# Two stacked float32r products for the scores, and inverse sums applied after the value product, in a two-layer hybrid encoder step

## The chip, the cores and the metric

One core of a Trainium2 chip runs the whole step. The metric is the device time of one execution in microseconds (us). The kernel before was run three times; the times given are the median and the extremes. The names used here: TensorE (PE) multiplies matrices, VectorE (DVE), ScalarE (ACT) and GpSimd (POOL) work on vectors, SyncE (SP) only issues transfers.

## The reference, cut to what matters

A two-layer encoder takes 1024 prompt frames and 8 streams of 16 frames. Each layer projects the normalised input into the operands of three groups of heads, attends, projects back and runs an MLP:

```
z = rmsnorm(x) @ W_in
A  "fox": 4 heads x 64, causal:      softmax(q k^T/8 + cum_q - cum_k) v      (forgetting attention)
B  "mla": 8 heads, q and k from latents, 64 + 32 rotary: softmax(q k^T / sqrt(96) + chunk mask) v
C  "swa": 4 q heads / 2 kv heads x 64, window of 3 chunks of 64, bias, a sink per head:
   softmax([q k^T/8 + bias, sink]) v
x = x + concat(A, B, C) @ W_out;   x = x + relu(rmsnorm(x) @ W_up)^2 @ W_down
```

Keys and values of the new frames are outputs too.

## The kernel before, in words

The frames are 9 tiles of 128 rows: 8 of the prompt and one with the 8 x 16 stream frames. Large products are made of three float32r (f32r) products, high x high, high x low and low x high: ScalarE rounds an operand to its high part, another engine subtracts to get the low part.

**Input projection.** The columns of W_in come in four slabs (512, 260, 416 and 512 wide), each in four weight pieces. Slab 0 holds fox queries and keys, slab 1 fox values and the forget gate, slab 2 the latents, slab 3 swa. Piece 4s+j of slab s is loaded by SP, rounded by ScalarE (in_hi, L1186) and its low part is made by VectorE (L1638) or GpSimd. ScalarE takes each product out of PSUM (evac_z); for slabs 0 and 3 into a staging tile, from which it issues the store of the keys (L1239) and which TensorE transposes a tile later (L2098, stg_bits). VectorE copies the transposed tile (stg_copy, L1649 to L1655) into qkTf or qkTs, [128, 4 or 3 planes, 1152 frames], where two heads share the 128 partitions of a plane. stg_copy runs inside VectorE's loop over tiles for slab 0, before the latents for six tiles of slab 3, and within the loop that normalises the latents (L1704, L1706) for the last three, at t = 2, 5 and 8.

**Latent stage.** After that loop VectorE copies the transposed latents (latT, L1716), ScalarE the rotary key (kTm, L1301), and TensorE sums the forget gates (L2188). SP meanwhile loads tables and masks and stores the new values, latents and gates, all from one queue, in written order.

**Prompt attention.** A hand-written list of 91 units per layer; a unit is some heads of one kind for one query tile (73 of them), or half of the tile's MLA query projection. Every engine walks the same list in steps. In step i TensorE transposes the probabilities of unit i-3 (LAG_T), multiplies the scores of unit i, and multiplies the values of unit i-4 (LAG). Transposed probabilities go in chunks of up to four 128 x 128 blocks through PSUM banks 4 and 5; VectorE copies even chunks (L1736), ScalarE odd ones (L1312), into ptb. In step i VectorE first copies its chunks, then normalises unit i-2 (LAG_N), and then takes the maxima of unit i. Normalising is one reciprocal of the row sums and, for each head, a multiply of its probabilities (L1748), and norm_ok releases the transposes. ScalarE takes the exponentials with row sums (sm_done) and copies the finished values out of PSUM (L1357) into omixT.

**Scores (L2237).** Queries and keys are plain f32. For fox and swa, whose planes hold two heads, GpSimd copies the queries of a tile into zero-padded planes (qzf, qzs; L1022, L1027), so that one product over 128 partitions sees one head alone. They are double buffered by tile.

## Time and profile before

| | us |
|---|---|
| three runs, median (extremes) | 2810.1 (2809.98 to 2814.61) |
| the profiled execution | 2807.96 |
| its span, first to last instruction | 2806.0 |
| TensorE busy in it | 2695.5 (96%) |
| mean granted TensorE clock | 0.989 |

The profile is of one execution. Busy time is per engine; an engine's idle time is put down to what released it. Only the idle time of an engine that everything waits for costs time. Matmuls are pipelined and their ends are modelled, so the start of one to the start of the next says more than a duration.

### The profile page before, as it was taken

How to read it: one execution, taken by the hardware profiler on the slowest of the kernel's cores; microseconds unless marked ns; L12 is line 12 of the kernel's file. 1: busy time of each engine (PE TensorE's matmuls, PEld its weight loads, DVE VectorE, ACT ScalarE, POOL GpSimd, SP SyncE). 2: the span in 40 equal slices, each digit the busy share in tenths (PEclk: the TensorE clock that was granted, in tenths of full speed). 3: DMA queues.
4: the chain of work that ended last, by engine and by line, in shares of the span. 5: the costliest groups of instructions: out<-in, count | busy, mean ns of one | idle time of the engine just before them, and what ended most of it. 6: DMA issues, size and time to landing. Idle time of an engine off the chain costs nothing.

```text
span 2806.0 us, 39617 instructions
## 1 busy us (share of the span) xinstructions
PE 2695.5 (96%) x14966; PEld 2177.9 (78%) x14966; DVE 1698.6 (61%) x2196; ACT 1054.8 (38%) x1969; POOL 1050.4 (37%) x594
## 2 busy tenths in 40 slices
PE   8999999899999999999999999998999999999997
PEld 6986666787888887888879756667878888878886
DVE  4026777635564558778740377775355564688777
ACT  4225544423323332333332255554243233333333
POOL 1112000114545457767511210001146444667766
PEclk9999999999999999999999999999999999999999
DMA  4212001432333446444132200013413433654441
GB/s 145 63 29 61 25 18 44 137 135 98 124 139 126 150 173 251 142 138 134 61 115 64 66 24 17 17 50 131 163 70 139 157 118 140 238 195 143 143 142 75
DMA packets 164722, 308.75 MB, mean 110 GB/s; under 512 B 24720, under 2 KB 90416, under 8 KB 164592
## 3 DMA queue, kind: packets, MB, share of 16 engines
q1 hardware_dynamic: 161280, 303.59, 31.4%
q10 hardware_dynamic: 3312, 3.41, 0.4%
q8 instruction: 84, 1.38, 0.2%
q14 instruction: 46, 0.38, 0.0%
HBM read 207.40 MB, written 97.72 MB: 109 GB/s over the span
## 4 chain that ended last, share of the span: by engine, by line
PE 86%; DVE 8%; ACT 2%; issue 2%; POOL 1%; DMA 1%; SPq 0%; DVEq 0%; ACTq 0%; POOLq 0%
PE ps L2583 8%; PE ps L2587 8%; PE ps L2585 8%; PE ps L2493 7%; PE ps L2494 7%; PE ps L2495 7%; PE ps L2237 6%; PE ps L2104 6%; PE ps L2106 6%; PE ps L2105 6%; PE ps L2098 5%; PE ps L2310 3%; PE ps L2370 2%; PE ps L2204 1%; PE ps L2438 1%
## 5 line engine op out<-in xcount | busy, mean ns | idle before, releaser
L2583 PE MATMUL ps<-wq_hi,sa_hi 128*128 128x512 f32 x896 | 349.0, 390 | 5.3 <-DVE x L2034 5.3
L2587 PE MATMUL ps<-wq_hi,sa_lo 128*128 128x512 f32 x896 | 348.6, 389 | 0.0
L2585 PE MATMUL ps<-wq_lo,sa_hi 128*128 128x512 f32 x896 | 348.6, 389 | 0.0
L2034 DVE TENSOR_TENSOR x<-ps,x 128x1024 f32<-128x1024 f32 x224 | 266.7, 1215 | 119.5 <-PE ps L2587 115.4
L1082 POOL TENSOR_TENSOR wq_lo<-wsum,wq_hi 128x1024 fp32r<-128x1024 f32 x64 | 157.5, 2462 | 289.7 <-ACT wq_hi L1454 289.7
L1972 DVE TENSOR_TENSOR sa_lo<-ra,sa_hi 128x1024 fp32r<-128x1024 f32 x112 | 253.3, 2263 | 19.8 <-ACT sa_hi L1474 19.7
L2104 PE MATMUL ps<-w_hi,hT_hi 128*128 128x512 f32 (+2 forms) x672 | 248.1, 369 | 0.3 <-DVE hT_lo L1643 0.3
L2106 PE MATMUL ps<-w_hi,hT_lo 128*128 128x512 f32 (+2 forms) x672 | 246.1, 366 | 0.0
L2105 PE MATMUL ps<-w_lo,hT_hi 128*128 128x512 f32 (+2 forms) x672 | 245.1, 365 | 0.0
L1964 DVE TENSOR_TENSOR cq<-ps,cq 128x1024 f32<-128x1024 f32 x48 | 58.6, 1221 | 285.4 <-ACT cq L1515 243.2
L2493 PE MATMUL ps<-hT_hi,wq_hi 128*128 128x512 f32 x512 | 203.2, 397 | 7.6 <-DVE hT_lo L1928 7.6
L1088 POOL TENSOR_TENSOR wq_lo<-rq,wq_hi 128x1024 fp32r<-128x1024 f32 x64 | 170.3, 2673 | 107.5 <-ACT wq_hi L1465 107.5
L2495 PE MATMUL ps<-hT_hi,wq_lo 128*128 128x512 f32 x512 | 201.5, 393 | 0.0
L2494 PE MATMUL ps<-hT_lo,wq_hi 128*128 128x512 f32 x512 | 201.3, 393 | 0.0
L2583 PEld LDWEIGHTS ps<-wq_hi,sa_hi 128*128 128x128 f32 x896 | 168.2, 188 | 41.6 <-issue 7.1
L994 POOL TENSOR_TENSOR w_lo<-w_raw,w_hi 128x1024 fp32r<-128x1024 f32 (+2 forms) x32 | 71.0, 2222 | 335.4 <-ACT w_hi L1186 335.4
L2587 PEld LDWEIGHTS ps<-wq_hi,sa_lo 128*128 128x128 f32 x896 | 168.2, 188 | 35.3
L2585 PEld LDWEIGHTS ps<-wq_lo,sa_hi 128*128 128x128 f32 x896 | 168.2, 188 | 34.7
L1082 POOL TENSOR_TENSOR wq_lo<-rq,wq_hi 128x1024 fp32r<-128x1024 f32 x64 | 170.6, 2676 | 57.7 <-ACT wq_hi L1454 57.2
L1088 POOL TENSOR_TENSOR wq_lo<-bsum,wq_hi 128x1024 fp32r<-128x1024 f32 x64 | 157.3, 2469 | 88.4 <-ACT wq_hi L1465 88.4
L1515 ACT COPY cq<-ps 128x512 f32<-128x512 f32 x128 | 73.4, 588 | 277.7 <-PE ps L2495 161.3
L2493 PE MATMUL ps<-T_hi,wq_hi 128*128 128x512 f32 x384 | 150.3, 391 | 1.5 <-POOL wq_lo L1082 1.4
(323 smaller groups left out, 6188.1 us busy)
## 6 DMA issues: line engine op xcount, KB each, us to landing
ra<-hidden_scratch SPq DMA_DIRECT2D x112, 512.0 KB, 3.3
hidden_scratch<-cq SPq DMA_DIRECT2D x94, 512.0 KB, 2.7
rq<-in_w_up_dram SPq DMA_DIRECT2D x64, 512.0 KB, 3.9
rq<-in_w_down_dram SPq DMA_DIRECT2D x64, 512.0 KB, 4.3
residual_scratch<-x SPq DMA_DIRECT2D x27, 512.0 KB, 3.1
x<-residual_scratch SPq DMA_DIRECT2D x27, 512.0 KB, 7.3
x<-in_x_prompt_dram SPq DMA_DIRECT2D x16, 512.0 KB, 6.9
w_raw<-in_w_in_dram SPq DMA_DIRECT2D x16, 512.0 KB, 4.2
```

Source lines behind the costliest of these rows:

```text
L1082: nc.gpsimd.tensor_tensor(wq_lo[o % 4][:], up_source(o)[:], wq_hi[o % 4][:], ALU.subtract).then_inc(up_lo.sem, 1)
L1088: nc.gpsimd.tensor_tensor(wq_lo[k][:], down_b_source(o)[:], wq_hi[k][:], ALU.subtract).then_inc(b_lo.sem, 1)
L2034: nc.vector.tensor_tensor(part, bank(b0 + 2 * pair, 2).rearrange("p (t n) -> p t n", t=2), part, ALU.add).then_inc(dn_ev.sem, 1)
L2104: pe.matmul(out, ah, bh, start=(k == 0), stop=False)
L2105: pe.matmul(out, ah, bl, start=False, stop=False)
L2106: last = pe.matmul(out, al, bh, start=False, stop=(k == n - 1))
L2493: pe.matmul(out, wh[:, cols], h[:, k, :], start=new and k == 0, stop=False, skip_group_check=True)
L2494: pe.matmul(out, wh[:, cols], lo_h[:, k, :], start=False, stop=False, skip_group_check=True)
L2495: last = pe.matmul(out, wl[:, cols], h[:, k, :], start=False, stop=k == 3, skip_group_check=True)
L2583: pe.matmul(out, ah[:, k, :], bh[:, k * 512:(k + 1) * 512], start=new and k == 0, stop=False, skip_group_check=True)
L2585: pe.matmul(out, ah[:, k, :], bl[:, k * 512:(k + 1) * 512], start=False, stop=False, skip_group_check=True)
L2587: last = pe.matmul(out, al[:, k, :], bh[:, k * 512:(k + 1) * 512], start=False, stop=final and k == 1, skip_group_check=True)
```

## The change

1. **Scores.** For fox and swa one f32 product becomes two f32r products. VectorE's stg_copy makes a high part (rounded to f32r) and a low part (a subtraction) for tiles 0 to 7. A new tensor keysF (keysS) holds for every key head the high part in partitions 0 to 63 and the low part in 64 to 127; queriesF (queriesS) holds the query's high part twice (j = 0) and its low part twice (j = 1). So (q_hi, q_hi) against (k_hi, k_lo), plus (q_lo, q_lo) against the same, is the whole product. The parts get into place by transfers that ScalarE issues in store_split: per tile two stores of queries to scratch in DRAM and four moves of keys within SBUF. SP loads the stacked queries back, tile by tile. The tile of the streams is copied plainly into newF and newS, after all stores of its kind have landed. The padding by GpSimd goes.
2. **Softmax.** L1748 goes. VectorE makes the reciprocal only; GpSimd spreads it over 64 columns per head (ginv); TensorE transposes it with the unit's probabilities as extra "inverse" blocks; VectorE multiplies the value product by the transposed inverse into omixT, in place of ScalarE's L1357. Of a unit with more than two chunks the first two are transposed ahead of the next scores, the others behind.
3. MLA units have at most four heads (tile 0 had one of eight), and the final norm uses signals that exist.

The core of the diff:

```diff
 def tile_units(kind, t):
-    n = min(HEADS[kind], 1024 // head_stride(kind, t))
+    n = min(HEADS[kind], 4, 1024 // head_stride(kind, t))
...
+def inverse_blocks(u):
+    _, _, h0, heads = UNITS[u]
+    return heads // 2 if heads > 1 else h0 % 2
...
     blocks = [(g, b) for g in range(UNITS[u][3]) for b in key_blocks(u)]
+    blocks += [("inverse", k) for k in range(inverse_blocks(u))]
...
# SP
+                for i in range(2):
+                    sp.wait_ge(split_out[i].sem, split_out[i].at(l, 2 * SPLIT_TILES))
+                load_queries("fox", 0)
                 sp.wait_ge(kpe_ev.sem, kpe_ev.at(l, NPT))
                 load(kTm[64:96, 1:MLA_H, :], kTm[64:96, 0:1, :].broadcast_to([ROPE, MLA_H - 1, NPT * P]), kpe_all)
+                sp.wait_ge(lat_ev.sem, lat_ev.at(l, NT))
+                sp.wait_ge(prep_out.sem, prep_out.at(l, 16 * 10))
+                load_queries("swa", 0)
                 for t in range(NPT - 1):
+                    for kind in ("fox", "swa"):
+                        sp.wait_ge(sc_mm.sem, sc_mm.at(l, scores_behind(kind, t)))
+                        load_queries(kind, t + 1)
                     sp.wait_ge(o_ev.sem, o_ev.at(l, TILE_END[t]))
...
# POOL
+                for u, n in ATTN.items():
...
+                    pool.wait_ge(inv_ok.sem, inv_ok.at(l, n + 1))
...
+                    nc.gpsimd.tensor_copy(ginv[:, m % 4, g0:g0 + heads, :],
+                                          rinv[:, n % 4, 0:heads].unsqueeze(2).broadcast_to([P, heads, HD])
+                                          ).then_inc(spread_ok.sem, 1)
...
# ACT
+                def store_split(kind, t):
+                    m = t if kind == "fox" else NT + t
+                    act.wait_ge(stg_ev.sem, stg_ev.at(l, m + 1))
...
+                    done = split_out[t % 2]
+                    for j in range(2):
+                        part = (split_hi, split_lo)[j][kind][t % 2]
+                        act.dma_start(query_d[kind][t, :, j, :], part[:, 0:2, :]...).then_inc(done.sem, 16)
+                        for r in range(2):
+                            rows, half = slice(64 * r, 64 * r + 64), slice(64 * j, 64 * j + 64)
+                            if kind == "fox":
+                                act.dma_start(keysF[half, r:FOX_H:2, toks[t]], part[rows, 2:4, :].bitcast(F32)).then_inc(done.sem, 16)
+                            else:
+                                act.dma_start(keysS[half, r, toks[t]], part[rows, 2, :].bitcast(F32)).then_inc(done.sem, 16)
...
                     if t >= 1:
                         evac_z(t - 1)
+                    if t >= 4:
+                        store_split("fox", t - 4)
...
                 for s in range(1, 4):
...
+                    if s == 1:
+                        store_split("fox", 5)
                     in_hi(4 * s + 2)
+                    if s == 1:
+                        store_split("fox", 6)
                     in_hi(4 * s + 3)
+                    if s == 1:
+                        store_split("fox", 7)
...
                         evac_z(s * NT + t)
+                        if s == 3 and t >= 3:
+                            store_split("swa", t - 3)
...
+                store_split("swa", 6)
+                store_split("swa", 7)
                 for t in range(NT):
                     act.wait_ge(lat_ev.sem, lat_ev.at(l, t + 1))
...
# DVE
                 def stg_copy(m):
...
+                    if t == NPT:
+                        for i in range(2):
+                            dve.wait_ge(split_out[i].sem, split_out[i].at(l, SPLIT_TILES * (1 if m < NT else 2)))
+                        nc.vector.tensor_copy(new[:], src[:, 0:planes, :]).then_inc(stg_ev.sem, 1)
+                        return
+                    if t >= 2:
+                        dve.wait_ge(split_out[t % 2].sem, split_out[t % 2].at(l, splits_stored(kind, t - 2)))
+                    chain.link(nc.vector.tensor_copy(high, src[:, 0:planes, :]))
+                    nc.vector.tensor_tensor(low, src[:, 0:planes, :], high, ALU.subtract).then_inc(stg_ev.sem, 1)
...
-                        if t == NT + 1:
+                        if t == NT:
                             lo(6, 0, 2 * SLABS_IN[1][1])
                             lo(7, 1, 2 * SLABS_IN[1][1])
...
-                        chain.link(nc.vector.reciprocal(inv, sums))
-                        for g in range(heads):
-                            probs = pbuf[n % 4][:, g * w:(g + 1) * w]
-                            last = nc.vector.tensor_scalar(probs, probs, inv[:, g:g + 1], None, ALU.mult)
-                        last.then_inc(norm_ok.sem, 1)
+                        nc.vector.reciprocal(inv, sums).then_inc(inv_ok.sem, 1)
...
+                    if i >= LAG and group_ending(i - LAG) is not None:
...
+                        dve.wait_ge(pv_mm.sem, pv_mm.at(l, n + 1))
+                        nc.vector.tensor_tensor(omixT[t % 2][:, c0:c0 + pairs, :].rearrange("p k n -> p (k n)"),
+                                                bank(6 + n % 2)[:, 0:pairs * P],
+                                                ptb[ch % NPTB][:, i0:i0 + pairs * P],
+                                                ALU.mult).then_inc(o_ev.sem, 1)
...
# PE
+                            qs, keys = [queriesF[:, h % 2, j, h // 2, :].bitcast(F32R) for j in range(2)], keysF[:, h, :].bitcast(F32R)
...
-                            last = pe.matmul(out[:, c0:c1], q, keys[:, k0 + c0:k0 + c1], start=True, stop=not masked)
+                            for j, q in enumerate(qs):
+                                last = pe.matmul(out[:, c0:c1], q, keys[:, k0 + c0:k0 + c1], start=(j == 0),
+                                                 stop=(j == len(qs) - 1 and not masked))
...
-                    pe.wait_ge(norm_ok.sem, norm_ok.at(l, n + 1))
+                    pe.wait_ge(sm_done.sem, sm_done.at(l, u + 1))
...
+                            if g == "inverse":
+                                if b == 0:
+                                    pe.wait_ge(spread_ok.sem, spread_ok.at(l, n + 1))
+                                src = ginv_b[:, GROUP_OF[u] % 4, 2 * b:2 * b + 2, :].rearrange("p h d -> p (h d)")
...
-                        probs_transposes(i - LAG_T)
+                        probs_transposes(i - LAG_T, slice(0, 2))
                     if 3 <= i < len(UNITS):
                         scores(i)
+                    if transposing and len(chunks_of(i - LAG_T)) > 2:
+                        probs_transposes(i - LAG_T, slice(2, None))
```

## Rows read from the trace of the kernel before

**Rows 1.** The page's first lines: span, busy time and share of each engine.

```profile
span 2806.0 us, 39617 instructions
PE 2695.5 (96%) x14966; PEld 2177.9 (78%) x14966; DVE 1698.6 (61%) x2196; ACT 1054.8 (38%) x1969; POOL 1050.4 (37%) x594
```

**Rows 2.** Busy time by stretches: us, five engines with counts, TensorE clock, DMA share, GB/s.

```profile
200.00:220.00 20.00, 15.02 (x112) 14.40 (x110) 15.19 (x25) 3.03 (x12) 10.06 (x13) 0.83 0.69 180
220.00:518.00 298.00, 279.70 (x2091) 186.49 (x2092) 214.26 (x529) 155.91 (x422) 14.73 (x37) 0.99 0.12 35
1610.00:1908.00 298.00, 279.85 (x2097) 186.79 (x2096) 214.20 (x530) 155.91 (x422) 14.23 (x35) 0.99 0.12 35
```

**Rows 3.** Groups of TensorE instructions, 220 to 518 us: busy, mean ns | idle before.

```profile
L2098 PE MATMUL ps<-identR,pbuf_bits 128*128 128x128 f32 x492 | 60.0, 262 | 13.7 <-DVE pbuf L1748 11.3 <-ACT ptb L1312 2.1
```

**Rows 4.** The same view for VectorE and ScalarE, 220 to 518 us.

```profile
L1748 DVE TENSOR_SCALAR pbuf<-pbuf,rinv 128x256 f32<-128x256 f32 (+7 forms) x128 | 56.2, 476 | 2.6
L1748 DVE TENSOR_SCALAR pbuf<-pbuf,rinv 128x128 f32<-128x128 f32 x16 | 3.7, 298 | 0.1
L1736 DVE COPY ptb<-ps 128x512 f32<-128x512 f32 x72 | 49.4, 686 | 20.0 <-PE ps L2098 19.9
L1357 ACT COPY omixT<-ps 128x128 f32<-128x128 f32 (+2 forms) x49 | 14.1, 287 | 5.6 <-PE ps L2310 5.6
```

**Rows 5.** Timeline of TensorE: start, duration, line, tiles, shape, count.

```profile
234.31 7.13 PE L2254 MATMUL ps<-wukv,latT 128*128 128x512 f32 x16
260.93 0.88 PE L2098 MATMUL ps<-identR,pbuf_bits 128*128 128x128 f32 x8
261.64 3.69 PE L2237 MATMUL ps<-kTm,qTm 104*128 104x256 f32 x16
...
1452.05 0.46 PE L2104 MATMUL ps<-w_hi,hT_hi 128*128 128x512 f32 x1
1457.61 0.46 PE L2098 MATMUL ps<-identR,stg_bits 128*128 128x128 f32 x4
```

**Rows 6.** ScalarE's transfers of staged keys: ns min/median/max, first and last start, landing.

```profile
L1239 ACTq DMA_DIRECT2D out_dram<-stg x22: 338/338/411, 29.9 to 1591.3; - x22
...
DMA to landing us min/median/max: 1.5/1.7/8.7
```

**Rows 7.** Timeline of layer 1 where slab 1 starts, all engines.

```profile
1471.26 1.15 ACT L1186 CAST w_hi<-w_raw 128x520 fp32r<-128x520 f32 x2 [0.47 <-ACT stg L1223]
1471.99 1.44 DVE L1638 TENSOR_TENSOR w_lo<-w_raw,w_hi 128x520 fp32r<-128x520 f32 x2 [0.79 <-ACT w_hi L1186]
1472.74 0.39 PE L2133 MATMUL ps<-w_hi,hT_hi 128*128 128x260 f32 x1 [0.77 <-DVE w_lo L1638]
```

**Rows 8.** Timeline of layer 0's latent stage, all engines.

```profile
201.85 0.34 ACTq L1239 DMA_DIRECT2D out_dram<-stg  x1
201.90 8.08 SPq L661 DMA_DIRECT2D qTm<-const_mask_mla_q_dram  x2
206.45 0.54 DVE L1655 COPY qkTs<-ps 128x384 f32<-128x384 f32 x1
206.91 0.54 DVE L1716 COPY latT<-ps 128x384 f32<-128x384 f32 x1
207.89 0.70 PE L2098 MATMUL ps<-identR,zc_bits 128*128 128x128 f32 x4 [3.03 <-ACT kTm L1301]
225.56 0.49 PE L2237 MATMUL ps<-qkTf,qzf 128*128 128x128 f32 x2
```

**Rows 9.** Duration (ns min/median/max) of lines near to the added operations.

```profile
L1653 DVE COPY qkTf<-ps x18: 691/692/694, 36.0 to 1474.8; 128x512 f32<-128x512 f32 x18
L1027 POOL COPY qzf<-qkTf x32: 391/401/493, 219.8 to 1766.5; 64x256 f32<-64x256 f32 x32
```

**Rows 10.** DMA issues: transfer, queue, count, KB each, median us to landing.

```profile
out_dram<-stg ACTq DMA_DIRECT2D x4, 64.0 KB, 4.8
```

More of the change, by code:

```diff
@@ L476, in hybrid_step @@
         max_done = signal("max_done", NATTN)
-        qz_ok = signal("padded_queries_copied", 2 * NPT)
+        split_out = [signal(f"split_stored{i}", 2 * SPLIT_TILES) for i in range(2)]
+        queries_in = {kind: signal(f"queries_in_{kind}", 32 * NPT) for kind in ("fox", "swa")}
         has_waited = signal("dve_has_waited", 0)
@@ L1016, in _ @@
                                             ALU.mult).then_inc(lb_ok.sem, 1)
-                def pad_zeros(bufs, other):
-                    for buf in bufs:
-                        for r in range(2):
-                            nc.gpsimd.memset(buf[64 * r:64 * r + 64, other(1 - r), :], 0.0)
-                def pad_queries(dst, src, planes, t):
-                    for r in range(2):
-                        rows = slice(64 * r, 64 * r + 64)
-                        last = nc.gpsimd.tensor_copy(dst[t % 2][rows, planes(r), :], src[rows, 0:2, toks[t]])
-                    last.then_inc(qz_ok.sem, 1)
@@ L1348, in _ @@
                                        ).then_inc(wk_ev.sem, 1)
-                    if i >= LAG and group_ending(i - LAG) is not None:
-                        n = group_ending(i - LAG)
-                        kind, t, h0, _ = UNITS[GROUPS[n][0]]
-                        pairs = sum(UNITS[u][3] for u in GROUPS[n]) // 2
-                        act.wait_ge(pv_mm.sem, pv_mm.at(l, n + 1))
-                        if t >= 2 and n == TILE_END[t - 1]:
-                            act.wait_ge(mix_out[t % 2].sem, mix_out[t % 2].at(l, 16 * (t // 2)))
-                        c0 = {"fox": 0, "mla": 2, "swa": 6}[kind] + h0 // 2
-                        nc.scalar.copy(omixT[t % 2][:, c0:c0 + pairs, :].rearrange("p k n -> p (k n)"),
-                                       bank(6 + n % 2)[:, 0:pairs * P]).then_inc(o_ev.sem, 1)
                 def mix_high(t):
@@ L1789, in attention_step @@
                                                             ALU.subtract).then_inc(max_done.sem, 1)
+                    if i >= LAG and group_ending(i - LAG) is not None:
+                        n = group_ending(i - LAG)
+                        kind, t, h0, _ = UNITS[GROUPS[n][0]]
+                        pairs = sum(UNITS[u][3] for u in GROUPS[n]) // 2
+                        ch, i0 = inverse_place(i - LAG)
+                        if ch % 2:
+                            dve.wait_ge(pt_act.sem, pt_act.at(l, ch // 2 + 1))
+                        if t >= 2 and n == TILE_END[t - 1]:
+                            dve.wait_ge(mix_out[t % 2].sem, mix_out[t % 2].at(l, 16 * (t // 2)))
+                        c0 = {"fox": 0, "mla": 2, "swa": 6}[kind] + h0 // 2
+                        dve.wait_ge(pv_mm.sem, pv_mm.at(l, n + 1))
[3 more added lines that the diff above has]
+                                                ALU.mult).then_inc(o_ev.sem, 1)
                 for n in range(0, 24, 2):
@@ L2387, in stream_scores @@
                                     else:
-                                        last = add(S[rows, 256:384], q, qkTf[:, 2 + c, new], stop=(c == 1))
+                                        last = add(S[rows, 256:384], q, newF[:, 2 + c, :], stop=(c == 1))
                     elif kind == "swa":
@@ L2396, in stream_scores @@
                                 else:
-                                    last = add(S[rows, 128:256], q, qkTs[:, 2, new], stop=True)
+                                    last = add(S[rows, 128:256], q, newS[:, 2, :], stop=True)
                     else:
```

144 lines of the change are left out of this document (81 added, 63 removed).

## The prediction

> **What bounds the kernel now.** I began with the page's busy shares: TensorE is busy 2695.5 of 2806.0 us, 96%, and no other engine passes 61% [rows 1]. So an edit counts by what it does to TensorE's instructions and to the 110 us in which it stands still. The busy time by stretches of layer 0 says where that is [rows 2]: the latent stage (200 to 220) leaves 5.0 of 20 us idle at a granted clock of 0.83 (a mean; 1 is the upper level, 2.4 GHz), and the prompt attention (220 to 518) leaves 18.3 of 298 us. Layer 1's attention repeats this with 18.2, so I work out one layer and double it.
>
> Inside the attention the groups of TensorE instructions name the loss [rows 3]: 13.7 us stand before the transposes of the probabilities, and VectorE's normalising line L1748 released 11.3 of them. VectorE has 128 of those instructions, 56.2 us, beside its 49.4 us of copies [rows 4].
>
> **Part 1, the inverse sums.** VectorE loses the 56.2 us of L1748, ScalarE the 14.1 us of L1357 [rows 4]. Neither bounds the stretch, so this is worth only the wait it removes. The transposes now wait for the exponentials (sm_done), not the scaling: I take the whole 13.7 us as gone; 18.3, all idle time, is the upper end. What comes in:
> - TensorE transposes 64 "inverse" blocks. Eight transposes start 0.71 us ahead of what follows [rows 5], so one is 0.09 us: +5.8 us.
> - 26 more chunk copies (170 for 144), alternating between VectorE and ScalarE, at most 0.69 each, and 50 multiplies of values by inverses on VectorE. A small L1748 is 0.30 us, a 512-wide VectorE tensor operation that reads PSUM 0.69 [rows 4, 9]: 15 to 35 us. VectorE falls from 214 to some 182 to 202 of 298 us, so it still doesn't bound.
> - GpSimd's 74 spreads, 0.40 us each by its nearest row [rows 9], are hidden: it is busy 14.7 of 298 us. In its queue only the table fills after the last tile stand behind a waiting spread.
> - VectorE's wait for the values product ends its step; behind it stands the next step's chunk copy, for which transposes wait. Cover is the product itself, which TensorE runs last in that step. I cost this at nothing and keep half of the 13.7 us as the lower end (second rival).
>
> **Part 2, the score products.** 160 f32 products per layer become 320 f32r ones. Sixteen f32 products of 512 columns take 7.13 us, less 0.17 of modelled tail: 435 ns each. Twenty-four f32r products start 5.56 us before what follows them: 232 ns [rows 5]. A pair costs 464, 29 ns more: +4.6 us. MLA's f32 products stay. So part 1 and these pairs give 13.7 - 5.8 - 4.6 = 3.3 us of gain (ends: 6.9 - 10.4 = -3.5, and 18.3 - 10.4 = +7.9).
>
> Here a rule says otherwise. The Trainium skill, page "FP8 and Floating Point Precision", section "TensorE Precision Notes", gives true FP32 four passes through the array; by it two one-pass products would halve the time of one. The rows' ratio of the two is 1.9, so I price by the rows; the halving stands below as a rival.
>
> **Part 3, making the split.** Per tile VectorE's copy becomes a copy and a subtraction, 0.69 each [rows 9], and ScalarE issues six transfers. One issue takes 0.338 us, the landing typically 1.7 us from the issue [rows 6]: six hold ScalarE for 2.03 us. 96 go out per layer. In three places something waits.
> - A, start of slab 1. Now ScalarE rounds both weight pieces at 1471.26, VectorE subtracts at 1471.99, and TensorE has already stood still 0.77 us at 1472.74 [rows 7]. Six issues now stand before the first rounding and six before the second. VectorE's second subtraction ends 2 x 2.03 us later, about 0.2 hides in the present gap: +3.9 us. Nothing covers this; TensorE's order has no other work here.
> - B, end of slab 3. VectorE's normalising loop contains the last three staging copies. Now the last one runs at 206.45, the first latT copy at 206.91, and TensorE resumes at 207.89, behind ScalarE's kTm copy, after 3.03 us [rows 8]. In the changed kernel the copy of tile 7 waits for the stores of tile 5, issued after ScalarE's transfer at 201.85, so from 202.2 to 204.25. SP's mask loads issue from 201.90 to 210.0 [rows 8]; the longest landing of the staged keys' stores, 8.7 us, is of one issued here [rows 6]. I take the landing as 210; then 1.2 us for the pair of tile 7 (0.54 each, and their hand-over), 2.03 us for its own six transfers, an ordinary 1.7 us landing: the last staging copy, which waits for every store, starts at 215.0 in place of 206.45: +8.5 us. With ordinary landings throughout it is 204.25 + 1.4 + 1.2 + 2.05 + 1.7 = 210.6: +4.2. If tile 7's stores land beside SP's 1 MB store in 4.8 us, the median of the four 64 KB ones [rows 10], it is +11.6.
> - C, slab 0. The copy of tile t waits for the stores of tile t-2. The step is 6.5 us; an ordinary landing leaves it just in time: +0.4 (0 to 5, if four steps stall 1.2 us each).
>
> By the Trainium skill, page "DMA: Bandwidth & Descriptors", section "Issuing engines are not separate DMA queues", all issuers' transfers interleave on the same 16 engines and the sequencer's time is usually small beside the transfer. Then A would be near 0 and B 4.2, the sum 8.2 us smaller per layer. The rows speak against it for 64 KB pieces: 2.03 us of issue against 1.4 us from the issue's end to the landing.
>
> **What costs nothing.** The first fox queries are loaded from SP's queue behind the logf stores and are wanted at 225.56 [rows 8], both moved by B alike. SP's two waits for the splits stand in front of the kTm broadcast, wanted only by the MLA units. Later query loads wait for the scores of the tile before, with the other heads' units for cover, and hold back only the mix stores. MLA tile 0 as two units of four moves no work. The final norm's signals are only renamed.
>
> **Sum per layer:** A 3.9 + B 8.5 + C 0.4 - 3.3 = +9.5 us, +19.0 for two. The profiled run took 2807.96 us (span 2806.0, 1.96 outside) and lies 2.1 under the median of 2810.1. So 2827.0 against the profiled run, 2829 against the median: 0.7% slower.
>
> **Rivals.**
> - Faster: the transposes' wait is worth more than its idle time. Their 492 records add up to 60.0 us [rows 3], against 44.3 at 0.09 us each; the 15.7 us between may be waiting inside modelled ends. If half of it is, part 1 and 2 gain 18.3 + 7.9 - 10.4 = 15.8 per layer and the sum is 12.8 - 15.8 = -3.0: 2804, or 2796 with B at 4.2. It decides from 15.6 us of gain. Against it: modelled ends of pipelined instructions overlap anyhow. Chance 0.11.
> - Slower still: the wait for the inverse spread and VectorE's wait for the values take half of the old wait's place. 12.8 + 3.5 = 16.3 per layer: 2843. For it: VectorE already waits 19.9 us for transposes before its chunk copies [rows 4], so the two take turns. Chance 0.13.
> - No measurable difference: ordinary landings (B 4.2) and all idle time gone (7.9): +0.6 per layer, 2811. Chance 0.16.
> - The score products do halve. 52,224 columns (counted from the list of units) at 435/512 ns are 44.4 us per layer; a saving of 22.2 in place of a cost of 4.6 gives -17.3: 2775. Chance 0.02, as an f32r product would have to fall from 232 to 109 ns. This is what the first page's rule would give.
>
> **How the numbers follow.** The forecast, A and B as worked out, has the remaining 0.58: 2829. A measurement of this kernel can tell about 0.2%, 5.6 us, from no change: faster is 0.11 + 0.02 = 0.13, same 0.16, slower 0.58 + 0.13 = 0.71. The range runs from 2804 (the faster rival's nearer end) to 2848: 2843, and 2.4 us more per layer of the 3.1 by which B can exceed 8.5. Left out are 0.02 below, half of the first rival and some 0.1 above. Slower cases alone: 2816 to 2848.
>
> **What would show it.** Right: ScalarE's rounding at slab 1 some 2 and 4 us later with TensorE idle behind VectorE's subtraction; the first latT copy 4 to 12 us later behind a staging copy that waits for a transfer; f32r score pairs at 464 ns; idle time before the transposes well under 13.7 us. Wrong: slab 1 without a gap, latT copies within 2 us of now, or a new releaser (GpSimd's spread, VectorE's multiply) with more than 7 us before transposes or values.

## The result, and the profile after

The changed kernel takes 2858.9 us (median of four runs, 2858.0 to 2861.8) against 2812.4 us for the kernel before in the same comparison (2810.0 to 2815.3): a ratio of 1.0167, interval 1.0149 to 1.0184. It is slower, as forecast, but by 46.6 us where 19 were forecast, and outside the range. The profiled execution took 2861.83 us, span 2860.0, mean granted clock 0.974 (before: 2807.96, 2806.0, 0.989). The page's first lines, after, against [rows 1]:

```profile
span 2860.0 us, 40455 instructions
PE 2700.9 (94%) x15094; PEld 2208.9 (77%) x15094; DVE 1628.1 (57%) x2102; ACT 1056.7 (37%) x1897; POOL 1057.7 (37%) x662
```

TensorE's busy time rose by 5.4 us only, the span by 54.0. So by the page almost all of the loss is idle time. That sum hides two opposite changes, and a table by stage shows them. I built it from both timelines, taking as bounds the starts of TensorE's instructions that both kernels have (first product of a slab, first product of the streams' tile in slab 3, first product with wuq, the transposes of wukv at the attention's end, the first product of the mix), in us, layer 0 / layer 1. The last column is the part of the difference that is idle time of TensorE:

| stage | before | after | difference | of it idle |
|---|---|---|---|---|
| slab 0 | 63.4 / 60.7 | 70.0 / 67.1 | +6.6 / +6.4 | +4.4 / +3.9 |
| slab 1 | 27.2 / 27.2 | 36.8 / 36.8 | +9.6 / +9.6 | +6.0 / +6.3 |
| slabs 2 and 3 | 87.3 / 87.3 | 87.3 / 87.3 | 0 | 0 |
| latent stage | 24.6 / 24.5 | 38.8 / 40.0 | +14.2 / +15.5 | +13.7 / +13.8 |
| prompt attention | 289.4 / 289.3 | 277.5 / 275.2 | -11.9 / -14.1 | +0.3 / +1.1 |
| streams' attention | 71.0 / 71.0 | 80.7 / 79.3 | +9.7 / +8.3 | -1.0 / -0.9 |
| the rest | 824.6 / 836.5 | 825.0 / 835.4 | +0.4 / -1.1 | +0.1 / 0 |

With the 0.7 us ahead of layer 0's first product the layers add up to +29.3 and +24.7, the span's difference. Four stages lose, the attention gains. In the attention TensorE works some 12 to 15 us less, in slabs 0 and 1 and the streams' stage some 15 to 17 us more; the page's total shows neither.

**Slab 1 (A).** The timeline of layer 1 after, ScalarE's queue and then TensorE, against [rows 7]; a "q" marks an issue of a transfer, the bracket is idle time and who ended it:

```profile
1506.87 0.45 ACTq L1279 DMA_DIRECT2D query_scratch_fox<-splitF_hi  x1
1507.35 1.26 ACTq L1284 DMA_DIRECT2D keysF<-splitF_hi  x2
1508.65 0.61 ACTq L1279 DMA_DIRECT2D query_scratch_fox<-splitF_lo  x1
1509.29 1.26 ACTq L1284 DMA_DIRECT2D keysF<-splitF_lo  x2
1510.64 0.62 ACT L1210 CAST w_hi<-w_raw 128x520 fp32r<-128x520 f32 x1 [4.19 <-issue]
...
1514.58 0.63 ACT L1210 CAST w_hi<-w_raw 128x520 fp32r<-128x520 f32 x1 [3.31 <-issue]
```

```profile
1512.13 0.58 PE L2197 MATMUL ps<-w_hi,hT_hi 128*128 128x260 f32 x1 [4.50 <-DVE w_lo L1682]
...
1516.06 0.59 PE L2197 MATMUL ps<-w_hi,hT_hi 128*128 128x260 f32 x1 [2.26 <-DVE w_lo L1682]
```

The mechanism is the one forecast: six issues before each rounding, VectorE's subtraction behind it, TensorE idle. The price is not. From 1506.87 to the rounding at 1510.64 the six take 3.77 us, 0.63 each, where I had 0.338. And idle time is not all: the windows of slab 1 in layer 1, before and after, show the granted clock at 0.86 in place of 1.00 and TensorE 3.3 us longer at the same products. From within the first of the two waits on it stood at 0.50 for 10.2 us, so of the 9.6 us lost 6.3 are idle time and 3.3 are clock.

```profile
1470.30:1497.50 27.20, 26.43 (x223) 26.21 (x223) 2.79 (x4) 6.72 (x21) 3.96 (x2) 1.00 0.23 68
```

```profile
1505.97:1542.78 36.81, 29.72 (x222) 29.00 (x222) 4.77 (x7) 6.72 (x21) 3.96 (x2) 0.86 0.34 94
```

**Slab 0 (C).** VectorE's split waits for the transfers of two tiles earlier. The transfers' own line says how often, and the timeline shows one of them:

```profile
L1284 ACTq DMA_DIRECT2D keysF<-splitF_hi x32: 603/623/1884, 50.3 to 1518.4; - x32
...
  DVE splitF_hi L1705: 52.0, 10
```

```profile
1490.03 0.69 DVE L1705 CAST splitF_hi<-ps 128x512 fp32r<-128x512 f32 x1 [5.59 <-DMA keysF<-splitF_lo]
```

The median issue is 623 ns; ten splits waited 5.2 us each on average. TensorE feels it as a wait for the low parts of the next tile's input: 4.3 us in three waits in layer 1 after, 0.3 us before.

**Latent stage (B).** The timeline of layer 0 after, VectorE, ScalarE, SP and TensorE, against [rows 8]:

```profile
218.78 8.15 SPq L691 DMA_DIRECT2D qTm<-const_mask_mla_q_dram  x2
228.18 0.56 DVE L1705 CAST splitS_hi<-ps 128x384 fp32r<-128x384 f32 x1 [6.62 <-DMA keysS<-splitS_lo]
229.72 2.80 ACTq L1286 DMA_DIRECT2D keysS<-splitS_hi  x2
232.56 1.35 ACTq L1279 DMA_DIRECT2D query_scratch_swa<-splitS_lo  x1
238.26 0.56 DVE L1700 COPY newS<-ps 128x384 f32<-128x384 f32 x1 [6.96 <-DMA keysS<-splitS_lo]
239.72 0.70 PE L2162 MATMUL ps<-identR,zc_bits 128*128 128x128 f32 x4 [13.55 <-ACT kTm L1355]
```

This is the forecast's chain: tile 7's split waits for tile 5's transfers until 228.18, its own six issues run from 229.36 to 235.21, the last copy starts at 238.26, and TensorE resumes after 13.55 us where it had 3.03. The six took 5.85 us, where I had 2.03. SP issues its masks from 218.78 on, in 8.15 us, and tile 5's last transfers, issued by 222.60, land 5.5 to 5.8 us after their issue; those of the tiles before mostly land 1.2 to 1.4 us after it.

**Attention.** Groups of TensorE's instructions in layer 0, after (251 to 530 us), against [rows 3], then the score groups of before (220 to 510 us):

```profile
L2162 PE MATMUL ps<-identR,pbuf_bits 128*128 128x128 f32 x492 | 60.3, 260 | 6.0 <-ACT ptb L1366 4.3 <-DVE ptb L1787 1.3
L2303 PE MATMUL ps<-keysF,queriesF 128*128 128x512 f32 (+3 forms) x96 | 23.7, 367 | 0.0
L2303 PE MATMUL ps<-keysS,queriesS 128*128 128x256 f32 (+1 forms) x64 | 9.4, 290 | 0.7 <-issue 0.7
L2162 PE MATMUL ps<-identR,ginv_bits 128*128 128x128 f32 x64 | 17.6, 312 | 4.4 <-issue 3.6 <-ACT pbuf L1387 0.6
L2383 PE MATMUL ps<-ptb,Vf 128*64 128x128 f32 x288 | 18.8, 277 | 2.3 <-ACT ptb L1366 2.1 <-issue 0.2
```

```profile
L2237 PE MATMUL ps<-qkTf,qzf 128*128 128x512 f32 (+3 forms) x96 | 37.2, 508 | 0.6 <-ACT pbuf L1333 0.6
L2237 PE MATMUL ps<-qkTs,qzs 128*128 128x256 f32 (+1 forms) x64 | 15.3, 382 | 0.7 <-issue 0.7
```

Read the counts first: 96 and 64 in both kernels, though the code now issues two products where it issued one. So **one f32 product is two records** in this profile. Before, 96 records were 48 fox products (four heads, and 12 pieces of at most 512 columns for each over the eight tiles); now they are 48 pairs. And the groups' busy time fell, from 37.2 to 23.7 and from 15.3 to 9.4 us. One head's 896 columns against one query tile show it, before and after:

```profile
417.31 1.74 PE L2237 MATMUL ps<-qkTf,qzf 128*128 128x512 f32 x4
418.88 0.22 PE L2239 MATMUL ps<-cmaskB,identB 128*128 128x128 bf16 x1
```

```profile
439.80 1.05 PE L2303 MATMUL ps<-keysF,queriesF 128*128 128x512 f32 x4
440.69 0.23 PE L2306 MATMUL ps<-cmaskB,identB 128*128 128x128 bf16 x1
```

From the start of the scores to the start of the mask it is 1.57 us as f32 (two pieces, four records) and 0.89 us as pairs (four products, four records).

**Streams' attention.** The forecast has no term for this stage. Busy time of it, before and after (us, five engines, clock, DMA share, GB/s):

```profile
509.36:580.35 70.99, 64.98 (x563) 56.06 (x562) 38.46 (x106) 29.44 (x75) 10.02 (x13) 1.00 0.31 106
```

```profile
528.55:609.24 80.69, 75.73 (x561) 64.89 (x562) 37.13 (x107) 29.03 (x74) 9.80 (x13) 0.85 0.28 93
```

The same instructions, 10.75 us more of them busy, at a clock of 0.85 in place of 1.00. Idle time hardly moved (6.0 to 5.0 us): this part of the loss is clock. It stands at 0.50 for 23.9 us of this stage, and before for none.

### The profile page after: what moved, and what is told of

Same layout as the page of the kernel before. It is cut to its first block, busy times and chain, and to the rows that moved or that the text cites. A ratio compares the mean times of both kernels' runs of the same rounds, so it can differ in the third digit from the quotient of the medians.

```text
span 2860.0 us, 40455 instructions
## 1 busy us (share of the span) xinstructions
PE 2700.9 (94%) x15094; PEld 2208.9 (77%) x15094; DVE 1628.1 (57%) x2102; ACT 1056.7 (37%) x1897; POOL 1057.7 (37%) x662
## 4 chain that ended last, share of the span: by engine, by line
PE 81%; issue 5%; DVE 5%; ACT 2%; ACTq 2%; DMA 2%; POOL 2%; SPq 0%; DVEq 0%; POOLq 0%
PE ps L2659 8%; PE ps L2663 8%; PE ps L2661 8%; PE ps L2569 7%; PE ps L2570 7%; PE ps L2571 7%; PE ps L2168 5%; PE ps L2170 5%; PE ps L2169 5%; PE ps L2162 5%; PE ps L2303 5%; PE ps L2383 4%; PE ps L2446 2%; PE ps L2268 1%; PE ps L2514 1%
## 5 line engine op out<-in xcount | busy, mean ns | idle before, releaser
L1073 POOL COPY ginv<-rinv 128x64 f32<-128x64 f32 (+2 forms) x148 | 41.2, 278 | 513.4 <-DVE rinv L1798 513.4
```

## The experiments

The kernel before was run again beside each set: 2813.1 us in the first, 2812.2 in the second, 2811.9 in the third. All times are medians unless said otherwise.

**First set: which part costs what.** *split_only*: the changed kernel with part 2 of the change taken back, that is normalising by VectorE as before, no inverse blocks, no spreads, ScalarE's copy into omixT; the limit of four heads for MLA and the new order of the transposes go back with it.

```diff
-                        nc.vector.reciprocal(inv, sums).then_inc(inv_ok.sem, 1)
+                        chain.link(nc.vector.reciprocal(inv, sums))
+                        for g in range(heads):
+                            probs = pbuf[n % 4][:, g * w:(g + 1) * w]
+                            last = nc.vector.tensor_scalar(probs, probs, inv[:, g:g + 1], None, ALU.mult)
+                        last.then_inc(norm_ok.sem, 1)
...
-                    pe.wait_ge(sm_done.sem, sm_done.at(l, u + 1))
+                    pe.wait_ge(norm_ok.sem, norm_ok.at(l, n + 1))
```

> The changed kernel with the inverse part undone: VectorE normalises the probabilities again (128 multiplies per layer), no inverse blocks, no spread, ScalarE copies the values out; the f32r pairs and everything that makes them stay. Theory (the pairs halve the score time, making the split is what costs): the input projection and the latent stage lose 31 us per layer as in the changed kernel, fox and swa scores gain some 20 us per layer, the wait for the normalising stays as before; the stream stage keeps its full clock. About 2812 + 2 x 11 = 2834 us. Rival (the inverse part made the gain in the attention, the pairs cost 4.6 us): about 2812 + 2 x 36 = 2884 us.

It took 2851.1 us, 1.0142 (1.0125 to 1.0159). Slabs 0 and 1 and the latent stage are as slow as in the changed kernel (67.8, 36.8, 39.2 us), the streams' stage is nearly as before (72.4, 72.6), and the attention is already 9.8 us faster than before (279.6, 279.5). The gain in the attention is mostly the pairs'. The total is 17 us above the 2834 expected, mainly because some 20 us per layer were expected there and 9.8 came: TensorE is busy 18.1 us less in it (254.9 for 273.0), but idle 8.2 us more (24.6 for 16.4).

*inverse_only*: the kernel before with the inverse part alone; plain f32 scores, padding by GpSimd between its spreads.

```diff
-                    pe.wait_ge(norm_ok.sem, norm_ok.at(l, n + 1))
+                    pe.wait_ge(sm_done.sem, sm_done.at(l, u + 1))
...
+                            if g == "inverse":
+                                if b == 0:
+                                    pe.wait_ge(spread_ok.sem, spread_ok.at(l, n + 1))
+                                src = ginv_b[:, GROUP_OF[u] % 4, 2 * b:2 * b + 2, :].rearrange("p h d -> p (h d)")
```

> The kernel before with the inverse part alone: zero-padded f32 queries by GpSimd as before, no split; sums inverted, spread by GpSimd, transposed with the probabilities, multiplied into the values by VectorE. Theory: 64 more transposes cost 5.8 us per layer and the idle time only moves from the normalising to the chunk copies and the inverse blocks, so the attention is 5 to 8 us longer per layer: 2822 to 2828 us, and 2841 to 2847 if the clock falls behind the attention here too. Rival (the removed wait pays): 13.7 - 5.8 = 8 us gained per layer, 2796 us.

It took 2823.8 us, 1.0036 (1.0016 to 1.0056). That is within the 2822 to 2828 expected, but by luck: the attention, which was to lose 5 to 8 us per layer, gained 0.5 in one and lost 1.5 in the other (288.9 and 290.8 us). The clock did fall behind it, for which 2841 to 2847 us was expected: the streams' stage takes 79.4 and 79.3 us. Groups of TensorE's instructions, 220 to 509 us:

```profile
L2134 PE MATMUL ps<-identR,pbuf_bits 128*128 128x128 f32 x492 | 60.0, 260 | 5.8 <-ACT ptb L1345 5.1 <-DVE ptb L1759 0.3
...
L2134 PE MATMUL ps<-identR,ginv_bits 128*128 128x128 f32 x64 | 16.7, 297 | 3.3 <-issue 2.5 <-ACT pbuf L1366 0.6
```

The idle time before the transposes falls from 13.7 to 5.8 us, but TensorE's whole idle time in the attention only from 16.4 to 13.5 us in layer 0 (288.9 less 275.4 busy) and from 16.3 to 12.4 in layer 1: the rest turns up before inverse blocks, values and MLA scores. TensorE's busy time rises by 2.4 and 5.4 us with 64 more transposes, so the two about cancel.

*sp_splits*: the changed kernel with the split's transfers issued from SP's queue, between its loads of weight pieces, and none from ScalarE's.

```diff
 # SP
-                for i in range(6, PC_IN):
+                for k in range(4):
+                    store_split("fox", k)
+                piece(6, in_piece(l, 1, 2))
+                store_split("fox", 4)
+                store_split("fox", 5)
+                piece(7, in_piece(l, 1, 3))
+                store_split("fox", 6)
...
+                for k in range(NPT):
+                    store_split("swa", k)
 # ACT
-                    if t >= 4:
-                        store_split("fox", t - 4)
...
```

> The changed kernel with the 96 transfers per layer issued from SP's queue, each tile's six as soon as VectorE has made its parts, none from ScalarE. Theory (ScalarE's issues and the stores that start late are the cost): slab 0 and the start of slab 1 return to the times of before, the latent stage to within 3 us, so 25 to 30 us are back per layer: 2800 to 2809 us. Rival (VectorE's second operation and the landings are the cost, whoever issues): more than 2840 us.

It took 2819.5 us, 1.0027 (1.0017 to 1.0037): some 39 of the 46.6 us are back with the queue, yet it is 10 us above the expected range. Slab 0 takes 63.4 and 61.1, slab 1 27.2, the latent stage 24.3 and 26.2 us, all within 2 us of before. The transfers and their bytes are the same, and so is the time of an issue: a median of 0.60 us on SP's queue as on ScalarE's. Two more things change with the queue, though. SP issues a tile's six as soon as its parts are made, and its masks go out behind the last of them, so that landings in the latent stage are back at 1.2 to 1.4 us from the issue's end. What each of the three is worth in slab 0 and in the latent stage this run doesn't separate. One new wait shows in TensorE's timeline of layer 0, the first scores waiting for the first queries from scratch, which SP loads behind its stores:

```profile
232.71 0.66 PE L2303 MATMUL ps<-keysF,queriesF 128*128 128x128 f32 x2 [7.03 <-DMA queriesF<-query_scratch_fox]
```

With it the attention takes 284.2 and 283.5 us, and the streams' stage is as slow as in the changed kernel (80.6, 77.2): that is what the expectation left out.

*warm*: the changed kernel with 12 more transposes, into a bank that is overwritten, where TensorE waits for ScalarE's wukT at the attention's end.

```diff
+                    for k in range(12):
+                        turned(bank(2, 2)[:, k % 8 * P:(k % 8 + 1) * P], wukv_b[:, k % 8].rearrange("p e d -> p (e d)"))
                     pe.wait_ge(wk_ev.sem, wk_ev.at(l, 1))
```

> The changed kernel with 12 more transposes of a resident tile, into a PSUM bank that is rewritten afterwards, where TensorE stands still 1.1 us for ScalarE's wukT copy at the end of the attention. Theory (the lower clock level at the start of the stream stage is set off by the idle time at the end of the attention): the granted clock stays at 1.00 behind it and the stream stage is 9 to 10 us shorter per layer: about 2840 us. Rival (the clock falls there whatever TensorE does in that gap, or falls later): 2857 to 2861 us, clock again near 0.85 in the stream stage.

It took 2849.6 us, 1.0133 (1.0116 to 1.015), against 1.0167; 2840 was expected. The profile is of the slowest of the four executions (2857.5), and in it the streams' stage takes 80.4 and 77.6 us, so it doesn't show where the other three gained. The first fall of the clock was gone, but it fell some us later, behind two short waits for ScalarE's kcT (0.72 and 0.79 us). One filled gap isn't the whole of it.

**Second set: what is queued behind VectorE's new wait, and the parts together.** *qlat_first*: the changed kernel, but in the attention's last step VectorE copies qpeS and the latent queries ahead of its wait for the last values product; the copies' later places go.

```diff
+                    if i == len(UNITS) + LAG - 1:
+                        nc.vector.tensor_copy(qpeS[0:ROPE].rearrange("p s h q -> p h s q"),
+                                              qTm[0][64:96].rearrange("p h (s q) -> p h s q", s=STREAMS)
+                                              ).then_inc(st_q.sem, 1)
+                        dve.wait_ge(ql_mm.sem, ql_mm.at(l, 1))
+                        nc.vector.tensor_copy(qlat[:].rearrange("p s h q -> p h s q"),
+                                              bank(2, 2).rearrange("p (h s q) -> p h s q", h=MLA_H, s=STREAMS)
+                                              ).then_inc(ql_ev.sem, 1)
                     if i >= LAG and group_ending(i - LAG) is not None:
```

> The changed kernel with one order on VectorE put back: in the last step of the attention it copies the stream queries (qpeS) and the latent queries (qlat) before it waits for the last values product, not behind it. Theory (TensorE stands still longer at the start of the stream stage because the latent queries stand behind VectorE's new wait, and that is where the clock is lost): one idle stretch of 0.6 to 0.8 us less per layer; if the clock then stays at its upper level the stream stage is 9 us shorter per layer, 2840 us; if the gap for wukT still sets it off, 2857 us. Rival (the order does not matter): 2857 to 2861 us and the clock again near 0.86 there.

It took 2849.9 us, 1.0132 (1.0114 to 1.015). That is halfway between the 2840 and the 2857 expected. The streams' stage falls to 75.1 and 77.7 us, its clock rises to 0.93 in layer 0. TensorE's wait of 0.66 us there, which the kernel before doesn't have, is gone, and so is the fall of the clock behind it; the fall behind the wait for wukT stays, and a short one comes later, from 553.4 on.

The next three take *sp_splits*' queue with one more step: SP waits for the splits and loads the first queries right behind the band, ahead of the stores of Vf and the rest. *sp_early_split* does that to *split_only*; *sp_early_qlat* to the changed kernel, with *qlat_first*'s edit; *sp_early_qlat_warm* adds *warm*'s.

```diff
 # SP, behind the load of the band
+                for i in range(2):
+                    sp.wait_ge(split_out[i].sem, split_out[i].at(l, 2 * SPLIT_TILES))
+                load_queries("fox", 0)
```

> The f32r pairs alone (VectorE normalises the probabilities as before, no inverse blocks), with the split's transfers issued by SP as soon as each tile is made, and the first fox queries loaded back before SP's stores of values, latents and gates. Theory (pairs halve the score products, ScalarE's issues were the cost, the inverse part only costs): projection and latent stage as before, attention 9.8 us shorter per layer as in the run with the pairs alone, stream stage within 2 us of before: 2812 - 16 to 20, 2792 to 2797 us. Rival (the split costs elsewhere too, for instance by VectorE's second operation): 2805 us or more.

> Both parts of the change, with SP issuing the split's transfers, the first fox queries loaded early, and VectorE's copies of the stream and latent queries put before its last values multiply. Theory: projection and latent stage as before, attention 12 us shorter per layer; stream stage 71 us if the clock holds (2786 us), 79 us if it does not (2802 us). Rival (the inverse part is worth keeping only if the attention is shorter than with the pairs alone): not below the run with the pairs alone.

> The same as the last with 12 more transposes in TensorE's gap before the latent queries. Theory (with both gaps closed the clock stays at its upper level): stream stage 71 us, about 2786 us, and below the run without the transposes if that one loses its clock. Rival (clock falls all the same): 2800 us or more.

They took 2796.1 us, 0.9944 (0.9927 to 0.9961); 2797.0 us, 0.9948 (0.9931 to 0.9964); and 2791.2 us, 0.9925 (0.9908 to 0.9941). All three beat both kernels; the last is the lowest of the study, though its interval overlaps the others'. The wait of 7.03 us is gone (latent stages 24.2 to 25.8 us). Where the first two differ is instructive: *sp_early_split* has 280.2 and 281.6 us in the attention and 72.6 and 70.8 in the streams' stage, *sp_early_qlat* 275.2 and 276.9, and 75.9 and 74.1. With VectorE's copies early, the inverse part earns about 5 us in the one stage and loses about 3 in the other; in the medians nothing of that is left (the second profile is of the fastest of its four executions, 2791.3). With *warm*'s transposes that stage is at 70.8 and 74.7. The page's head of the last kernel, and its streams' stage by windows in both layers:

```profile
span 2788.6 us, 40503 instructions
PE 2677.6 (96%) x15118; PEld 2189.9 (79%) x15118; DVE 1636.2 (59%) x2102; ACT 1056.1 (38%) x1897; POOL 1057.4 (38%) x662
```

```profile
498.43:569.27 70.84, 66.01 (x573) 57.08 (x574) 38.37 (x107) 28.96 (x74) 9.87 (x13) 1.00 0.32 106
1877.32:1951.98 74.66, 70.47 (x573) 60.79 (x574) 36.34 (x107) 28.87 (x74) 9.94 (x13) 0.93 0.30 101
```

**Third set: two questions left.** *late_stores*: the changed kernel with the three sets of issues at slab 1's start behind both roundings, still on ScalarE.

```diff
-                    if s == 1:
-                        store_split("fox", 5)
                     in_hi(4 * s + 2)
-                    if s == 1:
-                        store_split("fox", 6)
                     in_hi(4 * s + 3)
                     if s == 1:
-                        store_split("fox", 7)
+                        for t in range(5, NPT):
+                            store_split("fox", t)
```

> The changed kernel with one order on ScalarE altered: at the start of slab 1 it rounds both weight pieces first and issues the 18 transfers of fox tiles 5, 6 and 7 behind them. Theory (term A is ScalarE's issues ahead of the roundings): TensorE's wait for the weight pieces, 7.7 us, goes; the 18 issues, some 11.4 us, still keep ScalarE from taking slab 1's products out of PSUM, and two banks cover about 6 us of that: slab 1 takes 30 to 33 us in place of 36.8, 8 to 14 us less in all, 2845 to 2851 us. Rival (the slab is late because the landings are late): slab 1 stays at 36 to 37 us, 2857 to 2861 us.

It took 2863.8 us, 1.0174 (1.0151 to 1.0198), no better than the changed kernel, where 2845 to 2851 was expected; slab 1 takes 37.0 and 38.0 us. (The wait that was to go, 7.7 us in the expectation, is 6.8 in the rows of slab 1: 4.50 and 2.26.) TensorE in layer 1:

```profile
1507.22 0.39 PE L2194 MATMUL ps<-w_hi,hT_hi 128*128 128x260 f32 x1 [0.78 <-DVE w_lo L1679]
...
1520.38 0.59 PE L2165 MATMUL ps<-w_hi,hT_hi 128*128 128x260 f32 x1 [8.22 <-ACT ffz L1266]
```

The wait for the low parts is back to 0.78 us, as in [rows 7], and in its place TensorE waits 8.22 us until ScalarE, busy issuing, has taken the tile's products out of PSUM. So the outcome is about the rival's, but not for its reason, late landings: ScalarE was on the path of this stage at both places of the issues that were tried.

*one_product*: *sp_early_split* without the second product of each pair, so that the low parts of fox and swa queries are left out. This line is added for fox and for swa:

```diff
+                            qs = qs[:1]
```

> The pairs alone, issued by SP, as in the run with early queries, with the second product of each pair (the low parts of the queries) left out. Theory (a product of 512 f32r columns takes 232 ns, and 26,112 columns per layer are left out): fox and swa records halve, the score instructions of fox and swa take 11.8 us less per layer, and the attention is 5 to 12 us shorter than 281 us, as far as VectorE lets it: 2772 to 2786 us. Rival (a product costs what one record suggested, so that 52,224 columns are left out): 23 us less per layer in the score instructions.

One run: 2801.8 us, where 2772 to 2786 was expected. Groups of TensorE's instructions in the attention, *sp_early_split* and then this:

```profile
L2130 PE MATMUL ps<-identR,pbuf_bits 128*128 128x128 f32 x492 | 59.4, 261 | 19.4 <-DVE pbuf L1780 17.0 <-ACT ptb L1337 2.2
...
L2271 PE MATMUL ps<-keysF,queriesF 128*128 128x512 f32 x48 | 15.8, 429 | 0.0
```

```profile
L2130 PE MATMUL ps<-identR,pbuf_bits 128*128 128x128 f32 x492 | 60.8, 265 | 26.1 <-DVE pbuf L1780 23.7 <-ACT ptb L1337 2.2
L2273 PE MATMUL ps<-keysF,queriesF 128*128 128x512 f32 x24 | 10.2, 463 | 0.0
```

Half the products are half the records, 24 for 48: an f32r product is one record. The attention didn't get shorter, 280.4 and 280.5 us against 280.2 and 281.6. TensorE is busy 9.0 us less in layer 0 and idle 9.2 us more, most of it as a longer wait for VectorE's normalising, 17.0 to 23.7 us. With the pairs in, and without the inverse part, TensorE's work no longer sets the length of this stage. The streams' stage takes 75.6 us in both layers, 10.2 of them at a clock of 0.50, in an execution without the inverse part.

## Why the prediction was right in sign and wrong in size

Slower was right, and A, B and C are where it said. The forecast +9.5 us per layer stands against +29.3 in layer 0: A, B and C cost 17.6 more than forecast, the attention gave 8.6 more, and 9.7 came from a stage without a term. The sign is in part luck. Had only the pairs been priced right (20.7 saved, see part 2), the sum would have read 12.8 - 28.6 = -15.8 per layer, faster; two errors in opposite directions kept it right.

**The price of an issue (A, B and C), the step that failed first.** "One issue takes 0.338 us" came from [rows 6], where each issue stands by itself. Back to back they take 0.60 to 0.63 us in the median. It is not the kind of transfer: the same store of queries takes 0.44 us (fox) and 0.33 (swa) as the first of its six, 0.61 and 0.60 as the fourth. Single ones take longer, 1.3 to 1.5 us where SP issues at the same time in the latent stage, and up to 2.07 elsewhere. A measured 9.6 for 3.9, B 14.2 and 15.5 for 8.5, C about 6.5 for 0.4. B even passed its upper end of 11.6: in layer 0 its last staging copy came 6.4 us later than forecast, 3.8 by its own six issues (5.85 us for 2.03) and some 1.3 by each of the two landings. C passed its upper end of 5. The price of an issue is not all of A and C either. The sum had only idle time in it, but 3.3 to 3.6 us of A and 2.2 to 2.5 of C are TensorE working longer at the lower clock. *sp_splits* shows that issuing them on ScalarE is the cause of all three: the same transfers from SP's queue, at the same 0.60 us each, bring the three stages back. For A, where the order on ScalarE was tried as well, it is the time that ScalarE spends; for B and C that time, the late place in its order and B's meeting with SP's masks are not told apart.

The Trainium skill, page "DMA: Bandwidth & Descriptors", section "Issuing engines are not separate DMA queues", holds the sequencer's time for usually small beside the transfer. I weighed that rule and set it aside, and the runs go further against it: six issues took 3.77 us against 2.1 from a fox key's issue to its landing, and changing the queue was worth 39 us.

**Part 2, wrong in sign.** "Sixteen f32 products of 512 columns take 7.13 us ... 435 ns each": these were 16 records, and eight products of 870 ns. The same mistake made 160 products of 80, and the count of columns twice too large. A pair at 464 ns does not cost 29 more, it saves 406. By columns: 4 heads x 36 key blocks x 128 for fox and 4 x 15 x 128 for swa are 26,112, so 44.4 us become 23.7, 20.7 saved per layer against +4.6 forecast. The groups' busy time fell by 19.4 us (52.5 to 33.1), which agrees. So the rival to which I gave 0.02, that the score products halve, has the mechanism right; its argument against, that an f32r product would have to fall to 109 ns, rested on the same misreading. The Trainium skill, page "FP8 and Floating Point Precision", section "TensorE Precision Notes", gives true FP32 four passes through the array; the rows give 870 / 232 = 3.75 to 1, so the measurement comes near the page's four.

**Part 1, wrong in size.** I took the 13.7 us of idle time as gone. *inverse_only* shows that 3 to 4 us of TensorE's idle time go and the attention gains nothing. VectorE's normalising was one of several things that hold up the transposes; with it gone the chunk copies come last (5.4 of 5.8 us in the rows of *inverse_only*), and 3.3 us turn up before the inverse blocks, for most of which the rows name no releaser. The sign named beforehand, idle time before the transposes well under 13.7 us, came true without the gain that it stood for. On its own the part's net, +0.5 and -1.5 us, was near the lower end I kept (6.9 - 5.8 = 1.1). Only with the pairs in does it earn, about 2 to 5 us, since VectorE's normalising is then what is late.

**Why 20.7 us of cheaper scores gave 10.** *split_only* and *one_product* answer: a shorter product makes TensorE wait longer, mostly for VectorE. In *split_only* 18.1 us of work went and 8.2 us of idle time came; in *one_product* the next 9.0 us bought nothing. Pairs alone gave 9.8 us, and both parts 11.9 and 14.1. That is the sum "13.7 - 5.8 - 4.6 = 3.3" replaced: neither price was right, and the two gains don't add.

**The streams' stage, left out.** The sentence that failed is "VectorE's wait for the values product ends its step; behind it stands the next step's chunk copy ... I cost this at nothing". In the last step no chunk copy stands behind it but the copies of the streams' queries. Both layers lose, in *inverse_only* too (8.4 and 8.3 us), and hardly in *split_only* (1.4 and 1.6): it comes mostly with the inverse part. Not all of it does, as *one_product* loses 4.6 in each layer without that part. TensorE's timeline in layer 0 after, and the clock by windows around the same wait:

```profile
530.50 3.38 PE L2341 MATMUL ps<-qTm,wukT 64*128 64x128 f32 x16 [1.10 <-ACT wukT L1401]
538.74 0.28 PE L2162 MATMUL ps<-identR,ckv_c_bits 128*128 128x128 f32 x1 [0.72 <-ACT kcT L1437]
539.86 0.22 PE L2446 MATMUL ps<-winM,identB 128*128 128x128 bf16 x1 [0.66 <-issue]
```

```profile
529.00:530.00 1.00, 0.40 (x5) 0.26 (x4) 0.00 (x0) 0.58 (x2) 0.00 (x0) 1.00 0.00 0
531.00:532.00 1.00, 1.00 (x7) 1.00 (x7) 0.00 (x0) 0.00 (x0) 0.00 (x0) 0.50 0.00 0
```

Behind the 1.10 us wait the granted clock is 0.50, the 1.2 GHz level, and the 16 products take 3.38 us. The waits of 0.72 and 0.66 us are followed by a second stretch at 0.50, from 541.2 to 558.3. The kernel before had the same wait, 1.09 us, stayed at 1.00, and took 2.05:

```profile
511.30 2.05 PE L2274 MATMUL ps<-qTm,wukT 64*128 64x128 f32 x16 [1.09 <-ACT wukT L1347]
```

Queries copied earlier (*qlat_first*) give 5.6 and 1.6 us of the stage back, so VectorE's wait is shown to cost part of it. What work in the gap gives alone (*warm*) its profile doesn't show; the time fell by 9.4 us. Together, with the splits on SP, they bring layer 0 to 70.8 us at 1.00. Layer 1 stays at 74.7 and 0.93. Why the same gap lets the clock fall in one kernel and not in the other stays open.

**The other rivals.** "Slower still", 2843, priced the inverse part's new waits. These are real (the inverse blocks' 4.4 us, the values' 2.3), but the attention gained all the same, and the loss came from terms that this rival doesn't name. "Faster" rested on waiting hidden inside modelled ends. No run shows any: while the idle time before the 492 transposes went from 13.7 to 6.0 us, their records stayed at 60.0 and 60.3 us. "No measurable difference" needed ordinary landings and all idle time gone. The fox keys' landings were near ordinary, a median of 2.1 us; those of swa's tile 5 and the issues were not, and the attention's idle time is 16.8 us after (277.5 less 260.7 busy) against 16.4 before.

## What to carry to other kernels

Before pricing an instruction by its records, count records against the code: here one f32 product left two, which turned a halving into a cost. Price issues of transfers back to back, on the queue on which they'll stand, and put them on an engine that nothing on the path waits for: the same transfers, 96 in each layer, cost 39 us more in all on ScalarE than on SP. Where a wait is added, ask also what the clock does behind it: in slab 1 a third of the loss was clock. When a wait is removed, ask what is late next; of 13.7 us of idle time 3 to 4 were to be had, and of 20.7 us of cheaper products 10.

## What the runs showed of the hardware

An f32 product of 512 columns takes 870 ns and appears as two records of 435, an f32r product 232 ns and one record; 896 columns of scores took 1.57 us as f32 and 0.89 as a pair. An issue of a transfer on ScalarE took 0.33 to 0.60 us as the first of six and 0.60 to 0.63 in the median behind it, and 2.07 at most; on SP's queue the median of the same 192 was 0.60 as well. The granted clock fell to 0.50 behind an idle 1.10 us in one kernel and stayed at 1.00 behind 1.09 us in another, and the stage that follows was 8 to 10 us longer in the former. Within an idle 4.50 us in slab 1 it fell to 0.50 for 10.2 us, and the slab's products took 3.3 us longer.
